# State-space rotation: temporaries in PSUM, small copies on ScalarE, taps of all chunks in the feed-forward buffers, u read back one slab later

## The reference

```python
# s5_mixer, x is the RMS-normalised input, 64 groups of 16 channels, 64 states each
u = x.reshape(B, L, S5_GROUPS, S5_GROUP)
a_re, a_im = mag * cos(li * dt), mag * sin(li * dt)
bu_re = einsum('blgc,gpc->blgp', u, bb_re)          # bu_im alike
# linear recurrence over L: h[t] = a * h[t-1] + bu[t], complex, from h0
y = einsum('gcp,blgp->blgc', c_re, h_re) - einsum('gcp,blgp->blgc', c_im, h_im) + d * u
y = gelu(y)
a, g = split(y @ w_glu)                             # 1024 x 2048
out = a * sigmoid(g)                                # also h_re, h_im of the last token
```

## Time and profile before

| | |
|---|---|
| median of 3 runs | 1431.77 us (1430.11 to 1433.22) |
| the profiled execution's own time | 1433.83 us |
| its span, from the first to the last instruction | 1431.5 us |
| busy: TensorE, VectorE, ScalarE, GpSimd | 95%, 48%, 31%, 26% of the span |
| mean granted TensorE clock | 0.961 of 2.4 GHz |
| chain that ended last | TensorE 86%, VectorE 9% |

### The profile page before, as it was taken

How to read it: one execution, slowest core, us unless ns; L and a number is a source line. 1 busy time by engine, 2 the same in 40 slices (tenths; PEclk the granted TensorE clock), 3 DMA queues, 4 the chain that set the end, 5 groups by cost and what they waited for, 6 DMA issues and landing times.

```text
span 1431.5 us, 25466 instructions
## 1 busy us (share of the span) xinstructions
PE 1352.8 (95%) x10119; PEld 1305.7 (91%) x10119; DVE 688.9 (48%) x902; ACT 437.5 (31%) x648; POOL 367.3 (26%) x368
## 2 busy tenths in 40 slices
PE   4999999999999999999998577999999999999998
PEld 3999986779999999999998466999999999999998
DVE  6663334647774653432443878234443343333443
ACT  4311143423441331331421013422431331431423
POOL 3010013525899930000046652022100000000022
PEclk9999997999999999999999677799999999999999
DMA  5223230214222222223237833422222322323222
GB/s 141 74 74 86 75 88 18 59 36 101 77 84 85 78 85 87 84 77 88 80 92 153 101 78 74 110 87 86 77 84 78 88 79 83 88 74 87 87 75 81
DMA packets 239138, 119.53 MB, mean 84 GB/s; under 512 B 35512, under 2 KB 235888, under 8 KB 239088
## 3 DMA queue, kind: packets, MB, share of 16 engines
q1 hardware_dynamic: 238832, 118.78, 31.7%
q10 hardware_dynamic: 256, 0.06, 0.0%
HBM read 108.08 MB, written 10.73 MB: 83 GB/s over the span
## 4 chain that ended last, share of the span: by engine, by line
PE 86%; DVE 9%; issue 1%; ACT 1%; SPq 1%; DMA 1%; POOL 0%; DVEq 0%; ACTq 0%; POOLq 0%
PE ps L309 74%; PE ps L1552 2%; PE ps L1525 2%; DVE wlo L293 1%; PE ps L1705 1%; PE ps L1701 1%; PE ps L1515 1%; PE ps L1561 1%; PE ps L1555 1%; DMA raw<-in_ffn_w_down 1%; DVE R L330 1%; PE ps L1578 1%; PE ps L1643 0%; PE ps L1763 0%; DVE rot L1375 0%
## 5 line engine op out<-in xcount | busy, mean ns | idle before, releaser
L288 ACT ACTIVATE whi<-raw 128x1024 fp32r<-128x1024 f32 x177 | 187.1, 1057 | 524.7 <-PE ps L309 493.7
L309 PE MATMUL ps<-hid_hi,whi 128*128 128x288 f32 x1408 | 303.5, 296 | 10.9 <-DVE wlo L293 10.9
L309 PE MATMUL ps<-xg_hi,whi 128*128 128x288 f32 x1424 | 307.0, 296 | 3.1 <-DVE wlo L293 1.5
L309 PE MATMUL ps<-xg_hi,wlo 128*128 128x288 f32 x1424 | 304.7, 295 | 0.0
L309 PE MATMUL ps<-xg_lo,whi 128*128 128x288 f32 x1424 | 303.3, 294 | 0.0
L309 PE MATMUL ps<-hid_hi,wlo 128*128 128x288 f32 x1408 | 301.9, 296 | 0.0
L309 PE MATMUL ps<-hid_lo,whi 128*128 128x288 f32 x1408 | 301.1, 295 | 0.0
L293 DVE TENSOR_TENSOR wlo<-raw,whi 128x1024 fp32r<-128x1024 f32 x177 | 247.1, 1396 | 104.4 <-ACT whi L288 104.2
L309 PEld LDWEIGHTS ps<-hid_hi,whi 128*128 128x128 f32 x1408 | 226.6, 189 | 11.9 <-DVE wlo L293 6.8
L309 PEld LDWEIGHTS ps<-xg_hi,whi 128*128 128x128 f32 x1424 | 228.8, 189 | 5.1 <-issue 2.3
L309 PEld LDWEIGHTS ps<-xg_lo,whi 128*128 128x128 f32 x1424 | 228.8, 189 | 0.0
(11 more groups left out here) (347 smaller groups left out, 1199.6 us busy)
## 6 DMA issues: line engine op xcount, KB each, us to landing
raw<-in_ffn_w_up SPq DMA_DIRECT2D x64, 512.0 KB, 4.0
raw<-in_ffn_w_down SPq DMA_DIRECT2D x64, 512.0 KB, 3.7
raw<-in_mlstm_w_in SPq DMA_DIRECT2D x25, 512.0 KB, 3.8
raw<-in_s_w_glu SPq DMA_DIRECT2D x16, 512.0 KB, 4.0
raw<-in_mlstm_w_out SPq DMA_DIRECT2D x8, 512.0 KB, 3.7
MT<-d_taps SPq DMA_DIRECT2D x48, 64.0 KB, 2.5
d_u<-unat SPq DMA_DIRECT2D x8, 288.0 KB, 2.3
U<-d_u SPq DMA_DIRECT2D x16, 144.0 KB, 6.6
```

What stands on the lines that cost most here:

```text
L288: nc.scalar.activation(whi[:, s], raw[:, s], ACT.Copy).then_inc(whi_done, 1)
L309: last = nc.tensor.matmul(ps[:, 2 * s + c, 0:HN], w[:, s, k, :], a[:, k, c * HN:(c + 1) * HN], start=(k == 0 and n == 0), stop=(k == KT - ...
```

## The change

- **PSUM temporaries.** `states` keeps half of its temporaries in bank 0 (`A2`), and handles the real and the imaginary part in one instruction of 512 columns where it had two of 256. The factor of `normalised` lies in bank 1 (`R2P`). Every chunk's turned gains go through banks 2 and 3, so each waits for the evacuation of the one ahead.
- **Small copies.** The copies of `rho`, `h0` and `hP` move from VectorE to ScalarE (`columns`), with a semaphore `cols_ready` on which the scans, the answers and the turning of the end states wait. `rho` gets two buffers.
- **Taps.** The taps of all 8 chunks lie in the feed-forward buffers, each with a semaphore of its own; `MT` goes. Writing a chunk's hi or lo part waits until the taps in its place are used.
- **Order.** The first read-back of u is issued one slab later, behind the load of slab 96; the second one behind the taps of chunks 0 and 1. TensorE does the sums of i before it turns gains i+1.

```diff
+        taps_of = [late[:, k % 2, k - k % 2:k - k % 2 + 2].rearrange("p a n -> p (a n)")[:, 0:8 * P]
+                   .rearrange("p (g m) -> p g m", g=8) for k in range(KT)]
...
-        GB = (6, 2, 0, 2, 0, 2, 0, 2)
+        GB = (6, 2, 2, 2, 2, 2, 2, 2)
+        A2 = ps[:, 0].rearrange("p (r q c) -> p r q c", r=2, q=4)
+        R2P = ps[:, 1, 0:COLS]
...
-                sp.wait_ge(u_out, 16 * 4 * (half + 1))
+                sp.wait_ge(u_out, 16 * (KT if half else 5))
...
-                if k == 4:
+                if k == 5:
                     sp.wait_ge(taps_out, 16)
                     load_u(0)
...
-            load_u(1)
...
+            sp.wait_ge(slab_done, I_GLU)
             load_taps(0)
             load_taps(1)
-            sp.wait_ge(slab_done, I_GLU)
-            load_taps(KT - 2)
-            load_taps(KT - 1)
+            load_u(1)
+            load_taps(2)
+            load_taps(3)
...
-                    if k + 2 < KT - 2:
-                        load_taps(k + 2)
+                    if k + 4 < KT:
+                        load_taps(k + 4)
...
-                if k >= KT - 2:
-                    act.wait_ge(sy_done, KT)
+                act.wait_ge(sy_done, k - k % 2 + 1)
...
+            def columns(k):
+                g, s = slice(4 * k, 4 * k + 4), k % 2
+                if k >= 2:
+                    act.wait_ge(hst_ready, k - 1)
+                    nc.scalar.activation(hP[:, :, 4 * k - 8:4 * k - 4], Hst[:, s, :, :, COLS], ACT.Copy)
+                nc.scalar.activation(rho[:, s, :, 1:SP], s5s[:, MAG8, g].unsqueeze(2).to_broadcast([P, 4, SP - 1]), ACT.Copy)
+                if k >= 2:
+                    act.wait_ge(sy_done, k - 1)
+                nc.scalar.activation(Hst[:, s, :, :, 0:B], h0[:, :, :, g].rearrange("p r b g -> p r g b"),
+                                     ACT.Copy).then_inc(cols_ready, 1)
...
                     act.wait_ge(sy_done, k + 1)
+                    if k + 2 < KT:
+                        columns(k + 2)
                     nc.scalar.activation(U2[:, 8 * k:8 * k + 8, :]...
                 for k in GELUS.get(i, ()):
                     gelu(k)
+                if i == KT:
+                    act.wait_ge(hst_ready, KT)
+                    for k in range(KT - 2, KT):
+                        last = nc.scalar.activation(hP[:, :, 4 * k:4 * k + 4], Hst[:, k % 2, :, :, COLS], ACT.Copy)
+                    last.then_inc(cols_ready, 1)
...
-                V.tensor_copy(rho[:, :, 1:SP], s5s[:, MAG8, g].unsqueeze(2).to_broadcast([P, 4, SP - 1]))
-                V.tensor_tensor(rot[:, 0], vr, c, ALU.mult)
-                V.tensor_tensor(rot[:, 1], vi, sn, ALU.mult)
-                V.tensor_tensor(rot[:, 2], vi, c, ALU.mult)
-                V.tensor_tensor(rot[:, 3], vr, sn, ALU.mult)
-                own.link(V.tensor_copy(hN[:, :, :, g].rearrange("p r b g -> p r g b"), v0))
-                V.tensor_tensor(rot[:, 0], rot[:, 0], rot[:, 1], ALU.add)
-                V.tensor_tensor(rot[:, 2], rot[:, 2], rot[:, 3], ALU.subtract).then_inc(h_ready, 1)
-                V.tensor_tensor_scan(flat(rot[:, 1]), flat(rho[:]), flat(rot[:, 0]), 0.0, ALU.mult, ALU.add)
-                own.link(V.tensor_tensor_scan(flat(rot[:, 3]), flat(rho[:]), flat(rot[:, 2]), 0.0, ALU.mult, ALU.add))
-                V.tensor_tensor(rot[:, 0], rot[:, 1], c, ALU.mult)
-                V.tensor_tensor(rot[:, 2], rot[:, 3], sn, ALU.mult)
-                V.tensor_tensor(rot[:, 1], rot[:, 1], sn, ALU.mult)
-                own.link(V.tensor_tensor(rot[:, 3], rot[:, 3], c, ALU.mult))
-                V.tensor_tensor(Hst[:, s, 0, :, B + 1:], rot[:, 0], rot[:, 2], ALU.subtract)
-                V.tensor_tensor(Hst[:, s, 1, :, B + 1:], rot[:, 1], rot[:, 3], ALU.add)
-                own.link(V.tensor_copy(Hst[:, s, :, :, 0:B], h0[:, :, :, g].rearrange("p r b g -> p r g b")))
-                V.tensor_copy(hP[:, :, g], Hst[:, s, :, :, COLS]).then_inc(hst_ready, 1)
+                if k:
+                    dve.wait_ge(hst_ready, k)
+                V.tensor_tensor(rot[:], v[:, :, :, B:COLS], c, ALU.mult)
+                V.tensor_tensor(A2, v[:, :, :, B:COLS], sn, ALU.mult)
+                V.tensor_copy(hN[:, :, :, g].rearrange("p r b g -> p r g b"), v[:, :, :, 0:B]).then_inc(h_ready, 1)
                 dve.wait_ge(h_ready, k + 1)
+                V.tensor_tensor(A2[:, 1], rot[:, 0], A2[:, 1], ALU.add)
+                own.link(V.tensor_tensor(A2[:, 0], rot[:, 1], A2[:, 0], ALU.subtract))
+                dve.wait_ge(cols_ready, k + 1)
+                V.tensor_tensor_scan(flat(A2[:, 1]), flat(rho[:, s]), flat(A2[:, 1]), 0.0, ALU.mult, ALU.add)
+                own.link(V.tensor_tensor_scan(flat(A2[:, 0]), flat(rho[:, s]), flat(A2[:, 0]), 0.0, ALU.mult, ALU.add))
+                own.link(V.tensor_tensor(rot[:], A2, c, ALU.mult))
+                own.link(V.tensor_tensor(A2, A2, sn, ALU.mult))
                 if k >= 2:
                     dve.wait_ge(sy_done, k - 1)
+                V.tensor_tensor(Hst[:, s, 0, :, B + 1:], rot[:, 1], A2[:, 0], ALU.subtract)
+                V.tensor_tensor(Hst[:, s, 1, :, B + 1:], rot[:, 0], A2[:, 1], ALU.add).then_inc(hst_ready, 1)
...
                 dve.wait_ge(hhi_done, HID0[1] - KT + 1 + k)
+                dve.wait_ge(sy_done, k - k % 2 + 2)
                 V.tensor_tensor(hid_lo[:, k], yv[:], hid_hi[:, k].bitcast(F32), ALU.subtract).then_inc(hid_ready, 1)
...
-                elif k >= 3:
-                    pe.wait_ge(gt_ready, k - 1)
+                elif k >= 2:
+                    pe.wait_ge(gt_ready, k)
...
+                pe.wait_ge(cols_ready, k + 1)
+                pe.wait_ge(mt_in[k], 16 * T)
...
             for i in range(KT + 1):
+                if i < KT:
+                    block_sums(i)
                 if 0 < i < KT - 1:
                     gains_turn(i + 1)
-                if i < KT:
-                    block_sums(i)
                 if i:
                     answers(i - 1)
             pe.wait_ge(pool_pre, 1)
+            pe.wait_ge(cols_ready, KT + 1)
```

More of the change, by code:

```diff
@@ L154, in build @@
                 gtmp = sb("gtmp", [P, 4, T * GC], stack=s5_run)
-                rot = sb("rot", [P, 4, 4, SP], stack=s5_run)
-                rho = sb("rho", [P, 4, SP], stack=s5_run)
+                rot = sb("rot", [P, 2, 4, SP], stack=s5_run)
+                rho = sb("rho", [P, 2, 4, SP], stack=s5_run)
                 Hst = sb("Hst", [P, 2, 2, 4, COLS + 1], stack=s5_run)
@@ L177, in build @@
             GT = sb("GT", [P, 2, 8, P], stack=s5_a)
-            MT = sb("MT", [P, 2, 8, P], stack=s5_a)
             hN = sb("hN", [P, 2, B, GP], stack=s5_a)
         yn, yv = (sqb[:], R[:]), acc
-        taps_of = [MT[:, k % 2] for k in range(KT - 2)] + [
-            late[:, i, KT - 2:KT].rearrange("p a n -> p (a n)")[:, 0:8 * P].rearrange("p (g m) -> p g m", g=8) for i in range(2)]
+        taps_of = [late[:, k % 2, k - k % 2:k - k % 2 + 2].rearrange("p a n -> p (a n)")[:, 0:8 * P]
+                   .rearrange("p (g m) -> p g m", g=8) for k in range(KT)]
         gains_by = (GS[:], cT[:].rearrange("p r (q j) c -> p r q (j c)", q=4))
@@ L250, in build @@
             "u_ready u_out row_sel r2_pe r2_act r2_ready un_ready")
-        (s5_set, gs_ready, gt_done, gt_ready, v_done, h_ready, hst_ready, sy_done, yev_ready, gel_done) = sems(
-            "s5_set gs_ready gt_done gt_ready v_done h_ready hst_ready sy_done yev_ready gel_done")
+        (s5_set, gs_ready, gt_done, gt_ready, v_done, h_ready, cols_ready, hst_ready, sy_done, yev_ready, gel_done) = sems(
+            "s5_set gs_ready gt_done gt_ready v_done h_ready cols_ready hst_ready sy_done yev_ready gel_done")
         (ssend_pe, ssend_rows, sig_done, glu_done) = sems(
@@ L259, in build @@
             "fin_pe fin_act fin_ready xf_ready yt_done y_act y_dve y_out out_done")
-        raw_in, ps_free, c_in, c_out, u2_in, mt_in, late_in, yn_in, y2_out = (
+        raw_in, ps_free, c_in, c_out, u2_in, yn_in, y2_out = (
             [ctx.enter_context(nc.semaphore(f"{n}{s}")) for s in range(2)]
-            for n in ("raw_in", "ps_free", "c_in", "c_out", "u2_in", "mt_in", "late_in", "yn_in", "y2_out"))
+            for n in ("raw_in", "ps_free", "c_in", "c_out", "u2_in", "yn_in", "y2_out"))
+        mt_in = [ctx.enter_context(nc.semaphore(f"mt_in{k}")) for k in range(KT)]
         class Steps:
@@ L514, in _ @@
                     sp.dma_start(d_taps.rearrange("(k p) c -> p k c", p=P), ktap[:]).then_inc(taps_out, 16)
-            load_u(1)
             def load_taps(k):
-                s = k % 2
-                if 2 <= k < KT - 2:
-                    sp.wait_ge(sy_done, k - 1)
                 for i in range(T):
                     sp.dma_start(taps_of[k][i * GC:(i + 1) * GC],
-                                 d_taps[k * P:(k + 1) * P, i * GC:i * GC + P].rearrange("(g c) m -> c g m", c=GC)).then_inc(mt_in[s] if k < KT - 2 else late_in[s], 16)
```

(36 more changed lines are left out.)

1 line of the change is left out of this document (removed).

## The result

The changed kernel takes 1397.82 us (median of 4 runs, 1394.22 to 1399.91), the kernel before 1432.49 in the same comparison: ratio 0.9757, interval 0.9731 to 0.9782. That is 34.7 us less, where the sum said 35.5. A second set of five executions of the same kernel gave 1403.59 us (1397.44 to 1407.14), ratio 0.9811, interval 0.9792 to 0.9831, so 27.4 less than the kernel before beside it. The profiled execution, the fastest of the first set, took 1394.22 us (span 1392.4), 39.6 us less than the profiled one of before. Of these, 4.1 lie ahead of all changed lines (the same write of `unat` begins at 749.71 here and at 753.78 before), 0.5 around the span and 0.1 behind the GLU products; 34.9 are the changed stage.

The account below looks back on a forecast made before the run. TensorE was held up by VectorE's SBUF instructions stretched beside GpSimd, a slab wait and the low clock; -5.4 - 34.6 + 4.5 = -35.5 us took 1433.8 to 1398.3 (1396 beside the median), range 1388 to 1411.

Parts of the forecast that it names:

- the sum: Whole kernel: -5.4 at the read-back, -34.6 in the loop, +4.5 in the tail, together -35.5 us.
- The read-back: Before the last add into x: TensorE's 6.55 us wait goes, GLU slab late next; -5.4 us, bounds -8 and -3.
- VectorE's chain: States of each chunk: wider instructions, no small copies, all priced as uncontended; 5.8 us a chunk.
- The three rivals about PSUM: States: PSUM in place dearer, 1405, chance 0.13; still held up by GpSimd, 1421, 0.05; PSUM costs double, 1456, 0.05.
- the sum by the Trainium skill: States: extra fixed cost of PSUM sources makes 6.4 us of the 5.8, kernel some 2 us slower.
- ScalarE's copies: Three small copies per chunk ahead of the evacuation on ScalarE: 0.9 us, hidden under TensorE's next sums and transposes.
- The loop: The eight chunks replayed from t0: answers 7 end at +78.6 instead of +113.2, -34.6 us.
- the late hid_lo: VectorE's order ahead of states 5: hid_lo waits for ScalarE, TensorE waits 2.4 us, answers 5 run mostly at the lower clock.
- The tail: Behind answers 7: TensorE waits for ScalarE's last hP copies before turning the states, until +83.1; +4.5 us.
- Taps and order: DMA queue: all taps asked for without waiting for answers, landing before they are wanted; costed at nothing.
- lateness check: Taps of chunks 0 to 5: estimated landing times set against when they are wanted; a late one costs its lateness once.
- falls more often: Rival, TensorE clock in the loop: two more answers at the lower level, 1403; all of them, 1422; chance 0.20.

Follow-up runs that it names:

- the split and the lo parts: Changed kernel with VectorE's first-GLU-slab split behind the last add, and lo parts of chunks 0 and 1 behind states 5 and 6; 1386.4 us, ratio 0.9676.
- the split: Changed kernel with VectorE's split of the first GLU slab behind the last add and the squares instead of in front; 1392.9 us, ratio 0.9726.
- later lo parts: Changed kernel with the lo parts of chunks 0 and 1 one place later in VectorE's order, behind states 5 and 6; 1397.2 us, ratio 0.9757.
- transpose first: Changed kernel with TensorE's gain transpose ahead of the block sums again; 1403.2 us, ratio 0.9797.

## Why the prediction was right

**The read-back (-5.4).** In the profile -5.0: 787.75 - 778.66, less the 4.07 us that lie ahead. TensorE no longer waits for slab 96, and the GLU slab is late next, as said. ScalarE began on it 8.3 us after its issue (776.43 - 768.11); it was split from 777.5 on. Alone, in the kernel before, the same edit moved the median by only 2.9 us (interval of the ratio 0.9967 to 0.9993), so the size of this term rests on profiles.

**VectorE's chain (5.8 us a chunk).** 5.73 measured. Writing PSUM and working in place, which no row showed, cost 0.69 and 0.70 us, the lower bound. The three rivals about PSUM fall. So does the sum by the Trainium skill, "VectorE: DVE Perf Modes", section on the TRN2 errata: 6.4 us as an estimate from that page, against 5.73 in PSUM and 5.72 in SBUF without GpSimd. The cause, GpSimd, is shown by the kernel with the temporaries in SBUF.

**ScalarE's copies (0.9).** 0.22 + 0.40 + 0.30 us. Hidden, but no run shows a gain from moving them: with the copies on VectorE the kernel takes 1399.6 us, between its two sets. The prediction let them leave VectorE's chain without asking whether a later wait, the one for hid_hi, would take up what they cost there.

**The loop (-34.6).** From t0 + 113.2 to + 80.3: -32.9. Answers 0, the period of 6.8, the late hid_lo, the gap of 2.04 and answers 5 at 7.9 us came as written. Off by 1.7 us are answers 7, priced at the higher level: the prediction had them wait for states 7 alone, but an evacuation made TensorE wait 0.84 us ahead of them, and the level fell midway.

**The tail (+4.5).** 2.88: as answers 7 ended 1.7 us later, less of ScalarE's work was left to wait for. The two errors cancel, and that is luck: the prediction had the last evacuation wait for two gelus (until + 79.9), while in the trace it waited for answers 7 (until + 80.3). GLU products end at t0 + 98.2, + 98.0 was written.

**Taps and order, "at nothing".** True for the changed kernel, but not a free edit: without the early taps the loop of the profiled execution pays 4 us of waiting and 3.7 of clock. The prediction's lateness check covered only the new order.

**The clock.** The rival "falls more often" was weighed at 1403 for two more answers; the second set of the unchanged code lay at 1403.6. That the first set came within 1 us of the sum, and the second 8 us short of it, is therefore partly luck: the profile of either set's fastest execution has the pattern that the prediction wrote down, and of the slower ones there is no profile. Their mean granted clock is on record: over the nine of the changed kernel it falls from 0.975 at 1394.2 us to 0.966 at 1407.1 and never rises with the time. So the longer ones had more of the low level; in which answers, no profile shows. The kernel with the split and the lo parts, whose profile has no gap ahead of answers 5, is 11 us faster than the changed one's first set and 17 faster than the second, with clocks of 0.978 to 0.980, and spreads over 2 us, where the changed one's sets spread over 6 and 10.

## What to carry to other kernels

Two engines that slow each other in SBUF can be parted by giving one of them a PSUM operand: look in the trace for the same instruction beside and away from the other engine, and price the change by the quicker of the two. When an edit removes a wait of 2 us and the time hardly moves, look where the wait went and what TensorE's clock did behind it; here the profile of the later lo parts alone had the gap ahead of the next sums, and with the split there was none. And run the unchanged kernel beside each edit: against the first set the lo parts and the split gave 0.6 and 4.9 us alone and 11.5 together, against the second 6.4, 10.7 and 17.2. Whether they gain more together than the sum of both is not shown. That together they beat either alone is: their slowest run, 1386.9, lies below the fastest of either, 1391.4 and 1395.7.

## What was not expected of the hardware

- What a small SBUF copy costs on VectorE beside GpSimd's gains is not set by its size, nor is it one price, as the expectation had it (1.1 to 1.3 us each). With the copies on VectorE, `h0`'s 64 columns took 0.22 us in chunk 0 and 1.04 in chunk 2; `hP`'s 8 took 0.96 (1.16 in the next chunk) and 0.17 where no gains ran; a 256-column addition with one PSUM input took 0.43. Both of these `hP` copies ended with the GpSimd operation that ran beside them: 797.58 + 0.96 = 798.54, GpSimd's at 797.37 + 1.15 = 798.52; in the next chunk 807.06 and 807.03.

```profile
797.37 1.15 POOL L760 TENSOR_TENSOR gtmp<-bb,PW 128x512 f32<-128x512 f32 x1
```

- Answers 0 ran at the 1.2 GHz level in most profiles and at 2.4 in two: once behind the same work (later lo parts), once in the other order (transpose first). What decides it stays open. A higher level there need not save time, as with the later lo parts, where it brought a gelu ahead of its input.
- GpSimd is held up too when both work in SBUF: its operations take 1.10 to 1.60 us beside the temporaries in SBUF, 1.10 to 1.27 beside PSUM.
